# Feed-forward matmuls that alternate between output tiles

## The chip, the cores and the metric

The kernel runs on one core of a Trainium2 chip. The time is device microseconds of one execution. The core has TensorE (matmuls, in the profile PE, its weight loads PEld), VectorE (DVE), ScalarE (ACT), GpSimd (POOL) and SyncE (SP, which issues the DMAs). Each engine works through its own queue in order; they wait for one another through semaphores.

## What is computed

One step of a decoder of two layers, for 256 prompt tokens and 8 sequences of 8 new tokens: 320 columns in all, model width 1024. Each layer has a token mixer (gated linear recurrence beside sparse attention) and a feed-forward part. The change touches the latter alone:

```python
def conv_ffn(h, conv_past, w_gate_up, conv_w, conv_b, w_down):
    g, u = jnp.split(h @ w_gate_up, 2, axis=-1)
    ...
    conv = lax.conv_general_dilated(gfull, ...) + conv_b     # causal, 3 taps, per channel
    out = (jax.nn.gelu(conv) * u) @ w_down
    return out, gfull[:, -(CONV_W - 1):]
# per layer:
    ff, c_st = conv_ffn(rmsnorm(x, norm_ffn[l]), conv_past, ...)
    x = x + ff
```

The feed-forward width is 2816, 22 tiles of 128 channels.

## The kernel before, in words

Channels lie on partitions and the 320 tokens on the free axis. A float32 product is made of three products in fp32r: weights and activations are each split into a high part and a low part (the rest), and `split_products` (L773) issues high x high, high x low and low x high into one output tile. Each of them is one weight load and one matmul of 128x128 on 128x320. The sum over the input channels runs over eight (gate and up) or 22 (down) such triples, all into the same PSUM bank.

PSUM has eight banks, in two sets of four: `MM` (in the trace "mm") and `AXR` ("ax"). Each set is used in rotation by a plan written out by hand (`mm_plan`, `ax_plan`): a tile takes the bank of the tile four places before it in its plan, and `begin` (L689) makes TensorE wait until that one has been emptied. For gate and up the plan is g0, u0, g1, u1, ..., then dn0_0 to dn0_3. So g(j) and u(j) take the banks of g(j-2) and u(j-2), and the four tiles of the first half of down take those of g20, u20, g21, u21. The tiles of the second half, dn1_0 to dn1_3, lie in the other set, behind the last branch products and `norm2`.

Weights come by DMA into a ring of four slots. A part of a slot that is split at once is a unit. For gate and up a unit is both tiles j (2048 columns); for down it is two to four input tiles times four output tiles (1024 to 2048 columns). ScalarE writes a unit's high part (L1353, in the trace L1329 work_parts<-ring) into one of two buffers, once TensorE has read the unit two before; VectorE then puts the low part in the unit's place in the slot (L1690, in the trace L1693). TensorE waits for that (`w_low`) ahead of each unit.

TensorE's order in the feed-forward part (L1265 to L1303): for each of 22 passes j it waits for the unit, runs gate tile j (24 matmuls), then up tile j (24); behind gate tile 0 stands the sum of squares `norm2` (`square_sums`), from which ScalarE makes the scale of all the columns. Then come the units of down, first half (output tiles 0 to 3), then second half (4 to 7). In a unit the order is input tile k, in it output tile m, three products for each; only the last unit of a layer goes output tile by output tile.

In pass j VectorE (L2205 to L2234) splits unit j+1, multiplies gate by the scale (L2215, L2216, which empties the gate bank), makes the low part of the activation j-1 (`act_rest`, L2096), multiplies up by the scale (L2222, which empties the up bank), adds the two other taps of the convolution (L2226, L2228), and after the gelu takes the product with up (L2234). ScalarE (L1611 to L1626) makes the middle tap once gate is emptied, then the high part of unit j+2, then the gelu, then the activation's high part; in the first pass it has the logarithm and exponential of the scale ahead of these and a table load ahead of the gelu. GpSimd copies the borders of the convolution. For down, TensorE waits for activation k ahead of the first output tile of each input tile, in the first half.

The lines at which the order is set:

```python
for j in range(NJ):
    u = FFU + j
    pe.wait_ge(w_low[L], u + 1)
    split_tile(MM[L], f"g{j}", u, 0, h_high, h_low, (h_lo[L], 1) if j == 0 else None)
    if j == 0:
        square_sums()
    split_tile(MM[L], f"u{j}", u, 1, h_high, h_low)
```

Of the kernel before, what the change touches and what calls it, by code (L numbers as in the profile page):

```python
# [45 lines left out]
KD = D // P  # L46
SMP = NSEQ * STEPS
T = SEQ + SMP
DFF = 2816
NJ = DFF // P  # L50
# [183 lines left out]
def hybrid_step(nc, x_prompt, x_sample, cache_cmp, cache_slc, cache_win, state_hgrn, state_conv, page_table, norm_mix,  # L234
# [4 lines left out]
    with ctx:  # L239
# [61 lines left out]
        def part(buf, at, cols):  # L301
            return buf[:, at:at + cols]

        def heads(at):
# [22 lines left out]
        ring_r = nc.alloc_sbuf_tensor_at("ring_low", [P, NSLOT * SLOT], F32R, offset=ring_at)  # L327
# [5 lines left out]
        h_low = nc.alloc_sbuf_tensor_at("h_low", [P, KD * T], F32R, offset=hT_at)[:, :].rearrange(  # L333
            "p (k t) -> p k t", k=KD)
        h_high = part(work_r, 1280 + 2 * UNIT_COLS, KD * T).rearrange("p (k t) -> p k t", k=KD)
# [3 lines left out]
        act_high, act_low = (part(act_r, NJ * T * n, NJ * T).rearrange("p (j t) -> p j t", j=NJ) for n in range(2))  # L339
# [43 lines left out]
        def unit_of(u, buf):  # L383

            b, a, n = SPLIT[u]
            s = (BNO[b] % NSLOT) * SLOT
            if b[:2] in ("ff", "mg", "wo") or b in BY_HEAD:
                v = buf[:, s:s + SLOT].rearrange("p (k h c) -> p k h c", k=KD, h=4)
                return v[:, :, 2 * a:2 * a + 2, :] if b[0] == "w" else v[:, :, a::2, :]
            return buf[:, s + 512 * a:s + 512 * (a + n)].rearrange("p (k h c) -> p k h c", k=n, h=4)  # L390

        def unit_high(u):

            b, _, n = SPLIT[u]
            at = 1280 + UNIT_COLS * (u % 2)
            h = 4 if b[:2] in ("dn", "br") or b in ("w_hi", "w_kvn") else 2
            return work_r[:, at:at + n * h * P].rearrange("p (k h c) -> p k h c", k=n, h=h)
# [19 lines left out]
        def lsem(name):  # L417
            return [sem(f"{name}_{l}") for l in range(DEPTH)]
# [4 lines left out]
        h_hi, h_lo, stored = lsem("h_high"), lsem("h_low_ready"), lsem("outputs_stored")  # L423
        mm_full, mm_act, mm_dve = lsem("mm_full"), lsem("mm_emptied_by_act"), lsem("mm_emptied_by_dve")
# [12 lines left out]
        conv_ready, gelu_ready, act_ready = lsem("conv_ready"), lsem("gelu_ready"), lsem("act_ready")  # L437
# [12 lines left out]
        MM, AXR = [], []  # L450
# [235 lines left out]
        def _(pe):  # L686
            L = 0

            def begin(R, name):  # L689
                w = R.vacant(name)  # L690
                if w:
                    pe.wait_ge(*w)
                return R.bank(name)

            def mm(out, lhsT, rhs, start, stop):
                return nc.tensor.matmul(out, lhsT, rhs, start=start, stop=stop)  # L696

            def tr(out, in_):
                return nc.tensor.transpose(out, in_, ident[0:in_.shape[0], 0:in_.shape[0]])  # L699
# [73 lines left out]
            def split_products(out, high, low, x_high, x_low, start, stop):  # L773

                mm(out, high, x_high, start, False)
                mm(out, high, x_low, False, False)
                return mm(out, low, x_high, False, stop)

            def split_tile(R, name, u, h, x_high, x_low, tile_ready=None, between=None):

                bank = begin(R, name)
                kn = SPLIT[u][2]
                for k in range(kn):
                    if tile_ready is not None:
                        pe.wait_ge(tile_ready[0], tile_ready[1] + k + 1)
                    if between is not None and k == kn // 2:
                        between()
                    last = split_products(bank[:, 0:T], unit_high(u)[:, k, h, :], unit_of(u, ring_r)[:, k, h, :],
                                          x_high[:, k, :], x_low[:, k, :], k == 0, k == kn - 1)
                last.then_inc(R.full, 1)  # L790
# [290 lines left out]
            def layer(l):  # L1081

                nonlocal L
                L = l
# [30 lines left out]
                for x in range(2):  # L1115
                    bank = begin(AXR[L], f"kt{x}")
                    if x == 0:
                        pe.wait_ge(k_roped[L], 3)
                    for i in range(3):
                        last = tr(bank[:, P * i:P * i + TM[i]], stok[0:TM[i], i, 256 * x:256 * x + P])  # L1120
# [6 lines left out]
                banks = [begin(AXR[L], "hidk"), begin(AXR[L], "hidv")]  # L1127
# [7 lines left out]
                for j in range(16):  # L1135
                    for v in range(2):
                        rows = cmpT[:, j % 8, 2 * v:2 * v + 2, :, j // 8:j // 8 + NCB].rearrange(
                            "p g s n -> p (g s) n")
                        last = mm(banks[v][64 * v:64 * v + 64, 0:2 * NCS * NCB], w1[:, v, j, :], rows, j == 0, j == 15)
                        if j == 15:  # L1140
                            last.then_inc(ax_full[L], 1)
                for hb in range(2):
                    bank = begin(AXR[L], f"gsel{hb}")
# [6 lines left out]
                bank = begin(AXR[L], "kcm")  # L1150
                pe.wait_ge(hid_ready[L], 2)
                w2 = slot("w_cmp")
                for g in range(KVH):
                    last = mm(bank[64 * g:64 * g + 64, 0:NCS * NCB], w2[0:64, 2048:2048 + ND],
                              hid[0:64, g].rearrange("p s n -> p (s n)"), True, True)
                last.then_inc(ax_full[L], 1)
                for n in range(3):
                    bank = begin(AXR[L], f"vc{n}")
                    for y in range(6):
                        q, g = (6 * n + y) // 2, (6 * n + y) % 2  # L1160
                        last = mm(bank[0:NCB, ND * y:ND * y + ND], hid[64:128, g, q, :], w2[64:128, 2048:2048 + ND], True,
                                  True)
# [3 lines left out]
                for h in range(HH):  # L1166
                    bank = begin(AXR[L], f"krt{h}")
                    for i in range(3):
                        last = tr(bank[0:TM[i], P * i:P * i + P], kL[:, h, P * i:P * i + TM[i]])
# [24 lines left out]
                for hb in range(2):  # L1194
                    pe.wait_ge(*landed_at(f"kv{hb}", l))
                    kv = slot(f"kv{hb}").rearrange("p (w s a c) -> p w s a c", w=2, s=4, a=2)
                    for x in range(4):
                        w, bp = x // 2, x % 2
                        bank = begin(AXR[L], f"skt{hb}_{x}")
                        for y in range(4):  # L1200
                            last = tr(bank[:, P * y:P * y + P], kv[:, w, 2 * bp + y // 2, y % 2, 0:P])
# [6 lines left out]
                    for c in (2 * hb, 2 * hb + 1):  # L1208
                        bank = begin(AXR[L], f"ds{c}")
# [4 lines left out]
                        for h in range(HH):  # L1214
                            last = mm(bank[:, P * h:P * h + P], krP[rows, h, c // 2, :],
                                      vH[rows, c // 2, P * h:P * h + P], True, True)
# [5 lines left out]
                    n = 4 + 2 * hb  # L1222
# [27 lines left out]
                for n in range(2):  # L1250
                    for y, src, low in ((1, oN_high, oN_low), (0, oH_high, oH_low)):
                        u = MGU + 4 * n + 3 - y
# [8 lines left out]
                for m in range(KD):  # L1261
                    u = WOU + m // 2
                    pe.wait_ge(w_low[L], u + 1)
                    split_tile(MM[L], f"wo{m}", u, m % 2, m_high, m_low, (m_lo[L], 0) if m == 0 else None)
                for j in range(NJ):  # L1265
                    u = FFU + j
                    pe.wait_ge(w_low[L], u + 1)
                    split_tile(MM[L], f"g{j}", u, 0, h_high, h_low, (h_lo[L], 1) if j == 0 else None)
                    if j == 0:
                        square_sums()  # L1270
                    split_tile(MM[L], f"u{j}", u, 1, h_high, h_low)
                for u in down_units:
                    b, a, kn = SPLIT[u]
                    mh, n = int(b[2]), int(b[4:])
                    R = (MM[L], AXR[L])[mh]
                    final = u == len(SPLIT) - 1
                    if u == len(SPLIT) - 2 and l + 1 < DEPTH:
                        params_turned(l + 1)
                    pe.wait_ge(w_low[L], u + 1)
                    k0 = sum(DOWN[mh][:n]) + a  # L1280
                    tiles = [(k0 + kk, m) for kk in range(kn) for m in range(4)]
                    for k, m in sorted(tiles, key=lambda t: t[1]) if final else tiles:
                        bank = begin(R, f"dn{mh}_{m}") if k == 0 else R.bank(f"dn{mh}_{m}")
                        if mh == 0 and m == 0:
                            pe.wait_ge(act_ready[L], k + 1)
                        last = split_products(bank[:, 0:T], unit_high(u)[:, k - k0, m, :],
                                              unit_of(u, ring_r)[:, k - k0, m, :],
                                              act_high[:, k, :], act_low[:, k, :], k == 0, k == NJ - 1)
                        if k == NJ - 1:
                            last.then_inc(R.full, 1)  # L1290
                        if final and k == NJ - 1 and l == DEPTH - 1:
                            if m == 1:
                                turned_back(0, (0, 1, 2, 3))
                                end_sums((0, 1, 2, 3))
                            if m == 2:
                                end_sums((4, 5))
                                turned_back(1, (4, 5))
                            if m == 3:
                                end_sums((6,))
                                turned_back(1, (6,))  # L1300
                    if u in down_inner:
                        last.then_inc(down_read[L], 1)
# [6 lines left out]
            for k in range(KD):  # L1309
                bank = begin(PRO, f"x{k}")  # L1310
                for i in range(3):
                    last = tr(bank[:, P * i:P * i + TM[i]], xin[0:TM[i], i, P * k:P * k + P])
                last.then_inc(pro_full, 1)
            bank = begin(PRO, "low")
            tr(bank[:, 0:16], attb[0:16, 0:P]).then_inc(pro_full, 1)
            params_turned(0)
            for l in range(DEPTH):
                layer(l)
# [1198 lines left out]
```

## Time and profile before

| | |
|---|---|
| median of 3 runs | 1156.46 us (1153.97 to 1159.42) |
| the profiled execution: time, span | 1153.79 us, 1152.0 us |
| granted TensorE clock, mean | 0.985 |
| TensorE matmuls busy | 1125.9 us, 98% of the span |
| weight loads busy | 1023.6 us, 89% |
| VectorE, ScalarE, GpSimd busy | 62%, 47%, 17% |
| HBM read and written | 156.16 MB, 12.46 MB |

The profile is one execution. Busy time of an engine is a mean over all stages, and matmuls overlap in the records (a matmul of 0.31 us starts every 0.15 us), so the pace is to be read from start times, not from durations. The chain of waits says which engine set the end. "L696" is the helper line through which all matmuls pass, L1329 the one of ScalarE; the names of the tiles tell them apart.

### The profile page before, as it was taken

What the parts mean: (1) busy time and instruction counts of PE and PEld (TensorE: products, weight loads), DVE (VectorE), ACT (ScalarE), POOL (GpSimd) and SP (SyncE); (2) the same over time, 40 slices, a digit from 0 to 9 for tenths busy, and PEclk for the clock granted to TensorE, in tenths of its full rate; (3) what the DMA queues carried; (4) which work ended last, traced back from release to release, by engine and by line L of the source; (5) the groups of instructions that cost most, each with busy time, mean ns of one, the idle gap of its engine ahead of it and who ended that gap; (6) DMA issues with size and microseconds to landing.
All of it is one profiled execution on the core that took longest, in us unless ns stands there. A gap on an engine that the chain in (4) does not pass through costs nothing.

```text
span 1152.0 us, 20868 instructions
## 1 busy us (share of the span) xinstructions
PE 1125.9 (98%) x8473; PEld 1023.6 (89%) x8473; DVE 710.1 (62%) x1305; ACT 545.8 (47%) x867; POOL 192.8 (17%) x318
## 2 busy tenths in 40 slices
PE   6999999999999999999999999999999999999997
PEld 5988766778999999999999787776899999999997
DVE  5798165557567777763578835545656677777343
ACT  4543365553356555542444335655434555555232
POOL 2156300012121000100024560000312101100000
PEclk8999999989999999999999999999899999999998
DMA  9556331347644444344456535223684444432411
GB/s 295 160 156 217 110 95 52 111 120 219 220 147 146 147 147 148 114 141 163 146 124 208 184 97 158 74 68 114 177 266 152 149 153 155 155 124 92 168 41 46
DMA packets 151749, 165.90 MB, mean 144 GB/s; under 512 B 31596, under 2 KB 114406, under 8 KB 151398
## 3 DMA queue, kind: packets, MB, share of 16 engines
q1 hardware_dynamic: 151654, 164.58, 45.6%
q8 instruction: 67, 1.10, 0.4%
q14 instruction: 28, 0.23, 0.1%
HBM read 156.16 MB, written 12.46 MB: 146 GB/s over the span
## 4 chain that ended last, share of the span: by engine, by line
PE 92%; DVE 3%; DMA 2%; ACT 1%; issue 1%; SPq 1%; DVEq 0%; ACTq 0%
PE mm L696 65%; PE ax L696 23%; PE ax L699 3%; DMA ring<-in_state_hgrn 1%; ACT mixb L1329 1%; DVE ring_low L1693 1%; DMA ring<-in_state_conv 1%; ACT work_parts L1329 0%; SPq L498 0%; DVE mixb L1848 0%; DVE mixb L2127 0%; DVE work_parts L2096 0%; PE mm L699 0%; DVE cstT L1755 0%; DVE mixb L1865 0%
## 5 line engine op out<-in xcount | busy, mean ns | idle before, releaser
L696 PE MATMUL mm<-work_parts 128*128 128x320 f32 (+1 forms) x1088 | 345.7, 318 | 6.4 <-DVE h_low L1687 4.1
L1693 DVE TENSOR_TENSOR ring_low<-ring,work_parts 128x2048 fp32r<-128x2048 f32 (+2 forms) x116 | 256.0, 2207 | 128.3 <-ACT work_parts L1329 127.9
L696 PE MATMUL mm<-h_low,work_parts 128*128 128x320 f32 x1024 | 321.0, 313 | 0.0
L696 PE MATMUL mm<-work_parts,ring_low 128*128 128x320 f32 x1024 | 317.2, 310 | 0.0
L1329 ACT ACTIVATE work_parts<-ring 128x2048 fp32r<-128x2048 f32 (+2 forms) x116 | 212.2, 1829 | 152.6 <-PE mm L696 82.4
L696 PEld LDWEIGHTS mm<-work_parts 128*128 128x128 f32 x1088 | 206.5, 190 | 13.0 <-issue 7.0
L696 PEld LDWEIGHTS mm<-h_low,work_parts 128*128 128x128 f32 x1024 | 194.5, 190 | 0.3
L696 PEld LDWEIGHTS mm<-work_parts,ring_low 128*128 128x128 f32 x1024 | 194.6, 190 | 0.0
L696 PE MATMUL ax<-act_parts,work_parts 128*128 128x320 f32 x544 | 126.1, 310 | 0.6 <-DVE ring L2118 0.6
L696 PE MATMUL mm<-act_parts,work_parts 128*128 128x320 f32 x480 | 117.2, 309 | 0.0
L696 PE MATMUL mm<-hT,ring 128*128 128x320 f32 x384 | 109.6, 437 | 0.0
L696 PEld LDWEIGHTS mm<-hT,ring 128*128 128x128 f32 x384 | 70.7, 190 | 28.4 <-issue 1.4
L696 PEld LDWEIGHTS ax<-act_parts,work_parts 128*128 128x128 f32 x544 | 92.1, 188 | 2.5 <-DVE ring_low L1693 2.2
L696 PE MATMUL mm<-act_parts,ring_low 128*128 128x320 f32 x304 | 93.9, 309 | 0.0
L696 PE MATMUL ax<-act_parts,ring_low 128*128 128x320 f32 x304 | 93.9, 309 | 0.0
L1329 ACT ACTIVATE attb<-attb,prm 128x256 f32<-128x256 f32 x88 | 41.3, 517 | 93.1 <-DVE attb L2216 93.1
L696 PEld LDWEIGHTS mm<-act_parts,work_parts 128*128 128x128 f32 x480 | 82.9, 188 | 0.4 <-DVE merged_low L2096 0.4
L2387 POOL TENSOR_TENSOR ring<-ring,mixb 128x1024 f32<-128x1024 f32 x8 | 15.2, 1912 | 250.8 <-PE ax L696 250.8
L696 PEld LDWEIGHTS ax<-act_parts,ring_low 128*128 128x128 f32 x304 | 57.1, 188 | 0.0
L696 PEld LDWEIGHTS mm<-act_parts,ring_low 128*128 128x128 f32 x304 | 57.1, 188 | 0.0
L1329 ACT ACTIVATE attb<-ax 128x512 f32<-128x512 f32 (+4 forms) x56 | 34.4, 675 | 41.9 <-PE ax L699 36.0
L2222 DVE TENSOR_TENSOR attb<-mm,work 128x320 f32<-128x320 f32 x44 | 21.6, 491 | 48.6 <-PE mm L696 48.6
(247 smaller groups left out, 1589.5 us busy)
## 6 DMA issues: line engine op xcount, KB each, us to landing
ring<-in_w_gate_up SPq DMA_DIRECT2D x44, 1024.0 KB, 7.0
ring<-in_w_in SPq DMA_DIRECT2D x10, 2048.0 KB, 7.9
ring<-in_w_in SPq DMA_DIRECT2D x18, 1024.0 KB, 5.9
ring<-in_w_down SPq DMA_DIRECT2D x8, 1536.0 KB, 6.7
ring<-in_w_out SPq DMA_DIRECT2D x4, 2048.0 KB, 13.2
ring<-in_w_down SPq DMA_DIRECT2D x4, 2048.0 KB, 7.9
ring<-in_w_in SPq DMA_DIRECT2D x32, 128.0 KB, 3.5
ring<-in_cache_cmp_kv SPq DMA_DIRECT2D x32, 128.0 KB
```

The costliest lines, as they stand in the source:

```text
L696: return nc.tensor.matmul(out, lhsT, rhs, start=start, stop=stop)
L699: return nc.tensor.transpose(out, in_, ident[0:in_.shape[0], 0:in_.shape[0]])
L1329: return nc.scalar.activation(out, in_, f, **kw)
L1693: V.tensor_tensor(unit_of(u, ring_r), unit_of(u, ring), unit_high(u).bitcast(F32), ALU.subtract).then_inc(*st.up(w_low[l]))
L2222: V.tensor_tensor(ut, bank[:, 0:T], rs[:, 0:T], ALU.mult).then_inc(*st.up(mm_dve[L]))
L2387: G.tensor_tensor(s0, s0, end.to_broadcast([P, NSEQ, HD]), ALU.mult).then_inc(*st.up(decayed[L]))
```

## The change

Two helpers are added. `across_tiles` issues the three products pass by pass: high x high into every tile of a list, then high x low into every tile, then low x high. `split_pair` does this for gate tile j and up tile j; both banks are asked for first, and both are reported full at the end. The sum of squares of the first pass stands behind the pair. In down, all units but a layer's last go input tile by input tile across the four output tiles, the four banks are asked for at the first input tile, and the wait for an activation stands ahead of that.

```diff
+            def across_tiles(banks, highs, lows, x_high, x_low, start, stop):
+
+                out = []
+                for n, (weights, x) in enumerate(((highs, x_high), (highs, x_low), (lows, x_high))):
+                    out = [mm(bank[:, 0:T], w, x, start and n == 0, stop and n == 2) for bank, w in zip(banks, weights)]
+                return out
+
+            def split_pair(names, u, x_high, x_low, tile_ready=None):
+
+                banks = [begin(MM[L], name) for name in names]
+                for k in range(KD):
+                    if tile_ready is not None:
+                        pe.wait_ge(tile_ready[0], tile_ready[1] + k + 1)
+                    ends = across_tiles(banks, [unit_high(u)[:, k, h, :] for h in range(2)],
+                                        [unit_of(u, ring_r)[:, k, h, :] for h in range(2)], x_high[:, k, :],
+                                        x_low[:, k, :], k == 0, k == KD - 1)
+                for last in ends:
+                    last.then_inc(mm_full[L], 1)
...
-                    split_tile(MM[L], f"g{j}", u, 0, h_high, h_low, (h_lo[L], 1) if j == 0 else None)
+                    split_pair((f"g{j}", f"u{j}"), u, h_high, h_low, (h_lo[L], 1) if j == 0 else None)
                     if j == 0:
                         square_sums()
-                    split_tile(MM[L], f"u{j}", u, 1, h_high, h_low)
...
-                    tiles = [(k0 + kk, m) for kk in range(kn) for m in range(4)]
-                    for k, m in sorted(tiles, key=lambda t: t[1]) if final else tiles:
+                    for k in range(k0, k0 if final else k0 + kn):
+                        if mh == 0:
+                            pe.wait_ge(act_ready[L], k + 1)
+                        ends = across_tiles([begin(R, f"dn{mh}_{m}") if k == 0 else R.bank(f"dn{mh}_{m}") for m in range(4)],
+                                            [unit_high(u)[:, k - k0, m, :] for m in range(4)],
+                                            [unit_of(u, ring_r)[:, k - k0, m, :] for m in range(4)],
+                                            act_high[:, k, :], act_low[:, k, :], k == 0, k == NJ - 1)
+                        last = ends[-1]
+                        if k == NJ - 1:
+                            for end in ends:
+                                end.then_inc(R.full, 1)
+                    for k, m in [(k, m) for m in range(4) for k in range(k0, k0 + kn)] if final else []:
```

## Rows read from the trace of the kernel before

**Rows 1.** The page: TensorE's share of the span, and the chain that ended last

```profile
PE 1125.9 (98%) x8473; PEld 1023.6 (89%) x8473; DVE 710.1 (62%) x1305; ACT 545.8 (47%) x867; POOL 192.8 (17%) x318
...
PE 92%; DVE 3%; DMA 2%; ACT 1%; issue 1%; SPq 1%; DVEq 0%; ACTq 0%
```

**Rows 2.** The chain in order of time, both layers: start us, us, what

```profile
350.22 190.07 PE mm L696 x1296
...
906.70 190.07 PE mm L696 x1296
```

**Rows 3.** Windows, TensorE: us, PE busy (x), granted clock, DMA share, GB/s

```profile
353.58:501.42 147.84, 147.84 (x1010) 1.00 0.40 132
```

**Rows 4.** Timeline, TensorE, passes 0 and 1: start us, us, line, operation

```profile
346.00 0.31 PE L696 MATMUL mm<-work_parts 128*128 128x320 f32 x1
...
349.52 0.70 PE L696 MATMUL ax<-mixb,consts 128*128 128x320 f32 x2
...
353.58 0.30 PE L696 MATMUL mm<-work_parts 128*128 128x320 f32 x1
```

**Rows 5.** Timeline, ScalarE, passes 0 and 1

```profile
350.26 0.53 ACT L1329 ACTIVATE work<-ax,epsb 128x320 f32<-128x320 f32 x1 [0.80 <-PE ax L696]
350.82 0.47 ACT L1329 ACTIVATE work<-work 128x320 f32<-128x320 f32 x1
...
353.78 1.92 ACT L1329 ACTIVATE work_parts<-ring 128x2048 fp32r<-128x2048 f32 x1 [0.55 <-PE mm L696]
355.72 1.28 ACT L1329 ACT_TABLE_LOAD   x1
357.02 0.47 ACT L1329 ACTIVATE attb<-attb 128x320 f32<-128x320 f32 x1
...
360.72 0.94 ACT L1329 ACTIVATE attb<-attb,prm 128x256 f32<-128x256 f32 x2 [2.19 <-DVE attb L2216]
361.56 1.90 ACT L1329 ACTIVATE work_parts<-ring 128x2048 fp32r<-128x2048 f32 x1
```

**Rows 6.** Timeline, VectorE, passes 0 to 2

```profile
357.52 0.49 DVE L2234 TENSOR_TENSOR attb<-attb 128x320 f32<-128x320 f32 x1 [1.95 <-ACT attb L1329]
357.93 2.29 DVE L1693 TENSOR_TENSOR ring_low<-ring,work_parts 128x2048 fp32r<-128x2048 f32 x1
360.13 0.42 DVE L2215 TENSOR_TENSOR attb<-mm,work 128x256 f32<-128x256 f32 x1
...
361.00 0.49 DVE L2222 TENSOR_TENSOR attb<-mm,work 128x320 f32<-128x320 f32 x1
361.69 0.48 DVE L2226 SCALAR_TENSOR_TENSOR attb<-attb,prm 128x256 f32<-128x256 f32 x1 [0.21 <-ACT attb L1329]
...
362.81 0.28 DVE L2228 SCALAR_TENSOR_TENSOR attb<-attb,prm 128x64 f32<-128x64 f32 x1
...
364.26 2.29 DVE L1693 TENSOR_TENSOR ring_low<-ring,work_parts 128x2048 fp32r<-128x2048 f32 x1
```

**Rows 7.** Timeline, TensorE, behind the longest wait for a DMA

```profile
246.68 0.87 PE L696 MATMUL ax<-ring,mixb 128*32 128x128 f32 x16 [2.19 <-DMA ring<-in_state_hgrn]
```

**Rows 8.** Timeline, ScalarE and VectorE in down: splits of units

```profile
506.89 1.50 ACT L1329 ACTIVATE work_parts<-ring 128x1536 fp32r<-128x1536 f32 x1 [0.63 <-PE mm L696]
...
508.42 1.76 DVE L1693 TENSOR_TENSOR ring_low<-ring,work_parts 128x1536 fp32r<-128x1536 f32 x1 [1.90 <-ACT work_parts L1329]
...
528.01 1.07 ACT L1329 ACTIVATE work_parts<-ring 128x1024 fp32r<-128x1024 f32 x1 [3.78 <-PE mm L696]
```

**Rows 9.** Timeline, TensorE and VectorE: first matmuls of down, up 21

```profile
501.42 0.45 PE L696 MATMUL mm<-act_parts,work_parts 128*128 128x320 f32 x2
...
501.62 0.49 DVE L2222 TENSOR_TENSOR attb<-mm,work 128x320 f32<-128x320 f32 x1 [1.68 <-PE mm L696]
```

**Rows 10.** Windows, TensorE, as rows 3, behind the wait of rows 7

```profile
247.00:253.00 6.00, 6.00 (x109) 0.50 1.07 253
253.00:257.00 4.00, 4.00 (x19) 0.50 0.11 32
```

## The prediction

> **What bounds the kernel now.** I read the page's busy shares first, then the chain, then the chain in order of time, then the matmuls' own start times. TensorE works for 98% of the span and has one weight load for each matmul; 92% of the chain that ended last lies on it [rows 1]. In order of time, each of the two feed-forward stages is one unbroken piece of 190.07 us and 1,296 matmuls [rows 2], at a granted clock of 1.00 [rows 3], the higher of the two levels (2.4 GHz). So nothing releases TensorE here: its pace is the time, and every new wait in front of it is paid in full. VectorE and ScalarE are busy for 62% and 47%; what matters is not that share but how much of their work lies between the end of one pass and the start of the pass after next.
>
> **The pace.** Between the first matmul of pass 1 and the first of the down projection lie 21 pairs of 48 matmuls: 501.42 - 353.58 = 147.84 us, so 146.67 ns each [rows 4, 9]. There a matmul changes bank once in 24. The down projection changes bank once in 3. Its units of 36 matmuls are timed by ScalarE, which starts a split when the unit before has been read: four of them take 528.01 - 506.89 = 21.12 us, or 144 matmuls of 146.67 ns [rows 8]. 48 bank changes against about 6 differ by less than the 0.01 us to which a row is written, so a change of bank costs or gives under 0.01/42 = 0.24 ns. That is the main reason for my forecast: if a matmul had to wait for the one before it in the same bank, the down projection would already run faster.
>
> **The change, part by part.** It touches 22 x 48 = 1,056 matmuls of gate and up per layer and 480 of the 528 in down (the last unit, 4 x 4 x 3 = 48, keeps its order), 3,072 in both layers.
> - Order of the products. No matmul or weight load is added or removed. The same weights no longer come twice in a row, but each matmul has its load already [rows 1]. Most likely 0 ns; by the bound above +-0.24 ns x 3,072 = +-0.7 us. The far bound is 320 columns at 2.4 GHz, 133.3 ns, which no row shows as a pace.
> - The gate tile of a pass is now filled together with the up tile, half a pass (3.52 us) later. What VectorE and ScalarE did to gate while TensorE worked on up must now fit in the pass after. The trace has this very case: in pass 1 VectorE comes late and does everything in one run. From its first read of gate (360.13) to the start of the split of the next weights (364.26) it takes 4.13 us, and the split 2.29, 6.42 in all [rows 6]. With 0.03 us for a hand-over (ScalarE's 357.02 + 0.47 to VectorE's 357.52 [rows 5, 6]), 6.45 us. TensorE wants these weights one pass of 7.04 us after the fill, less the 0.20 us by which it issues ahead of it (501.42 against 501.62 [rows 9]): 6.84. Slack 0.39 us, so no wait in the steady passes. Cost 0; what hides it is the pass itself, and 0.39 us is all there is to lose.
> - The first pass of a layer. The sum of squares (norm2) moves from behind gate 0 to behind up 0. Pass 0 starts at 346.00, so norm2 is issued at 346.00 + 7.04 = 353.04 in place of 349.52 [rows 4]. Pass 1 still starts at 353.58. The logarithm follows 0.74 us after norm2 (350.26 - 349.52 [rows 4, 5]): 353.78; the exponential 0.56 later, 0.47 long [rows 5]: 354.81. VectorE reads gate at 354.84. ScalarE's convolution start comes 0.59 after that read (360.72 - 360.13 [rows 5, 6]): 355.43, the split's high part 0.84 later: 356.27, the table load of the gelu 1.94 after that: 358.21, the gelu 1.30 later: 359.51 [rows 5]. The taps (ready 1.40 us after 356.40, by 361.69 to 362.81 + 0.28 [rows 6]) are earlier and hide. The product follows at 360.01, the split of unit 2 at 360.42, ready at 362.71 [rows 6], TensorE at 362.74. It wants it at 353.58 + 7.04 = 360.62. **Wait: 2.12 us.** Next late is unit 3: VectorE begins gate 1 at 360.42 + 2.20 = 362.62 (the step 357.93 to 360.13), done at 369.04, wanted at 362.74 + 7.04 = 369.78: no second wait.
> - The start of down. The four banks are now asked for before the first matmul. The fourth was up 21, which was filled last; until now it was asked for 9 matmuls (1.32 us) later, and gate 21 had half a pass. Fill at 501.62, VectorE reads up 0.87 us behind the start of gate and takes 0.49 (361.00 - 360.13 [rows 6]): 502.98, TensorE 503.01, wanted 501.42 [rows 9]. **Wait: 1.59 us.** Behind this wait stand all of down and nothing of another queue: the weight loads of the slots are released by ends of passes, which only shift. Unit 2 of down is split by 501.62 + 4.13 + 1.76 = 507.51 at the latest and wanted at 508.29. I take 1.76 from a split of that size [rows 8].
> - In the second half of down (banks of the other set) the tiles asked for are those of the branch products and norm2, long empty: 0. The four fills at the end of a half come within 4 matmuls in place of 9 before; their reader comes later: 0. The wait for an activation stays ahead of each input tile: 0.
> Sum: 2 x (2.12 + 1.59) = +7.4 us. On the profiled execution (1153.79, span 1152.00) that is 1161.2. The median of the three runs shown is 2.67 above it, so I put the forecast at 1156.46 + 7.4 = **1163.9 us**, +0.64%.
>
> **The clock.** A gap in front of TensorE can cost more than itself. After the longest one, 2.19 us [rows 7], the granted clock was 0.50, the lower level (1.2 GHz), from about 247 to 257 us [rows 10]. Around that gap stand small matmuls (128x128 on 32 columns of the array), here stand full ones; so I take 0. Bound: with dense work behind, as in 253 to 257, 4 us at the half clock lose about 4 x (1 - 0.55) = 1.8 us per gap (0.55 = 146.67 / 266.7, 320 columns at 1.2 GHz), 7.2 for four. The Trainium skill, "TensorE: Matmul & The Clock Gate", section on psum-queue depth-cycling, goes further: a kernel that cycled through its banks each iteration had its clock fall and rise again and again, from short idle times between groups. By that rule the steady passes too would lose. The trace does not agree so far: with four banks in rotation the clock is 1.00 over the whole stage [rows 3].
>
> **The rivals.**
> - *Clock* (0.07). The four new gaps each bring the half clock: 1163.9 + 7.2 = 1171.1. For it: both the drop above and its length; against: one core in dense work.
> - *Chain longer than the pass* (0.05). VectorE's run of 6.45 us decides from 6.84 on. If the splits or reads were 10% slower under new overlaps, 7.1 us, each of some 40 passes would wait 0.25 us: +10, 1174. Against it: pass 1 has the same overlaps already.
> - *Smaller waits* (0.17). If the table load ran before ScalarE's split chain, its 1.30 us would leave the first wait: 0.82 + 1.59 twice, +4.8, 1161.3, within 0.5%. Against it: it follows the split at once [rows 5].
> - *Banks matter after all* (0.09), the other side: two matmuls in a row into one bank hinder one another, and only true alternation frees them. At 133.3 ns a pair takes 6.40 us, but then VectorE's chain binds: a pass starts every 6.45 + 0.20 = 6.65 us, 0.39 less than 7.04. 20 passes x 0.39 = 7.8, down 480 x 13.3 ns = 6.4, two layers 28.4, less 7.4: 1156.5 - 21.0 = 1135.5. It decides from 7.4 / 3,072 = 2.4 ns per matmul on, ten times the bound of the pace. That compiled order stays as before is not a case of its own: TensorE takes matmuls in program order, and it would show as no change.
>
> **How the numbers follow.** The main case has 0.62. A measurement of this kernel can tell about 0.5%, 5.8 us, from no change. The main case is only 1.6 us beyond it, so of its 0.62 I give 0.06 to "same". Slower: 0.56 + 0.07 + 0.05 = 0.68; same: 0.17 + 0.06 = 0.23; faster: 0.09. The range goes from no waits at all (1156.0) to the clock rival (1171.1, rounded up to 1172.0); it leaves out the bank case and the long chain, 0.14, and the far ends of the clock case.
>
> **What would show it.** Right: in the chain, the stage in three pieces with about 2.1 us before pass 2 (releaser VectorE's split, L1693) and 1.6 before down (releaser VectorE's read of up, L2222), 7.04 us from pass to pass, 5.28 per unit in down, clock 1.00. Wrong: pairs under 7.00 us (banks matter), a wait at each pass (chain too long), 0.50 in the clock behind the gaps, or a table load ahead of the split.

## The result, and the profile after

| | before | changed |
|---|---|---|
| median of 5 runs | 1156.46 us (1153.97 to 1159.42) | 1162.44 us (1161.46 to 1167.69) |
| ratio | | 1.0068, 95% interval 1.0044 to 1.0091 |
| profiled execution, time | 1153.79 us | 1167.69 us |
| its span, its mean granted clock | 1152.0 us, 0.985 | 1165.9 us, 0.981 |

The change makes the kernel slower by 0.7%; forecast were 1163.9 us and +0.64%. The profiled execution is the slowest of its five, so its span is not the result, but its waits can be read. Lines of the code have moved: the split is L1721 (was L1693), the read of up L2250 (L2222), the read of gate L2243 (L2215), ScalarE's helper L1357 (L1329).

The page of the changed kernel: busy shares, the chain by engine, and the two groups of matmuls in which the new idle time lies (the first had 6.4 us of it before, the second none). Columns of a group: count, busy us, mean ns, idle time before, and what ended it:

```profile
PE 1133.7 (97%) x8473; PEld 1030.6 (88%) x8473; DVE 714.0 (61%) x1305; ACT 539.4 (46%) x867; POOL 192.9 (17%) x318
...
PE 90%; DVE 4%; ACT 2%; DMA 2%; issue 1%; SPq 1%; DVEq 0%; ACTq 0%
...
L696 PE MATMUL mm<-work_parts 128*128 128x320 f32 (+1 forms) x1088 | 289.6, 319 | 10.1 <-DVE ring_low L1721 5.7
...
L696 PE MATMUL mm<-act_parts,work_parts 128*128 128x320 f32 x480 | 98.6, 309 | 2.9 <-DVE attb L2250 2.9
```

The counts are those of [rows 1]: nothing was added or taken away. TensorE's share of the chain fell from 92 to 90%, and VectorE and ScalarE gained it. The chain in order of time shows where (start us, us, what; first layer's feed-forward part):

```profile
349.69 0.55 PE ax L696 x2
...
352.86 1.80 ACT work_parts L1357
354.68 1.28 ACT L1357
356.97 2.21 DVE ring_low L1721
359.23 143.51 PE mm L696 x959
504.34 38.95 PE mm L696 x264
```

The unbroken 190.07 us of [rows 2] have become three pieces. Between the sum of squares (349.69) and 359.23 the end of the kernel hangs on ScalarE and VectorE, though TensorE is still at work on pass 1 for most of it; and down begins anew at 504.34. TensorE's timeline around both waits, the first from the second layer and the second from the first (in brackets the idle time and its releaser):

```profile
921.32 0.46 PE L696 MATMUL mm<-work_parts,ring_low 128*128 128x320 f32 x2
923.66 0.56 PE L696 MATMUL mm<-work_parts 128*128 128x320 f32 x2 [1.89 <-DVE ring_low L1721]
```

```profile
502.42 0.46 PE L696 MATMUL mm<-work_parts,ring_low 128*128 128x320 f32 x2
504.34 0.38 PE L696 MATMUL mm<-act_parts,work_parts 128*128 128x320 f32 x1 [1.46 <-DVE attb L2250]
```

Two matmuls start every 0.295 us here, so without a wait the next would have started at 921.62 and 502.72. The waits cost 2.04 and 1.62 us, counted from start to start in this way; the bracket is shorter, since it counts from the end of the last matmul. The first wait's chain, on ScalarE (scale, high part of unit 2, table load, gelu):

```profile
350.27 0.53 ACT L1357 ACTIVATE work<-ax,epsb 128x320 f32<-128x320 f32 x1 [4.27 <-PE ax L696]
350.83 0.47 ACT L1357 ACTIVATE work<-work 128x320 f32<-128x320 f32 x1
351.92 0.93 ACT L1357 ACTIVATE attb<-attb,prm 128x256 f32<-128x256 f32 x2 [0.62 <-DVE attb L2244]
352.76 1.90 ACT L1357 ACTIVATE work_parts<-ring 128x2048 fp32r<-128x2048 f32 x1
354.68 1.28 ACT L1357 ACT_TABLE_LOAD   x1
355.98 0.47 ACT L1357 ACTIVATE attb<-attb 128x320 f32<-128x320 f32 x1
```

and on VectorE:

```profile
351.33 0.42 DVE L2243 TENSOR_TENSOR attb<-mm,work 128x256 f32<-128x256 f32 x1 [3.01 <-ACT work L1357]
...
356.48 0.49 DVE L2262 TENSOR_TENSOR attb<-attb 128x320 f32<-128x320 f32 x1 [2.19 <-ACT attb L1357]
356.89 2.28 DVE L1721 TENSOR_TENSOR ring_low<-ring,work_parts 128x2048 fp32r<-128x2048 f32 x1
```

VectorE sits idle for 3.01 us. Both tiles are full soon after norm2 starts, at 349.53, and from there on it waits for the scale alone. From norm2's start to TensorE's restart it is 923.66 - 913.97 = 9.69 us in the second layer (norm2 started at 913.97); the prediction's steps add up to 362.74 - 353.04 = 9.70.

One thing is not as forecast: the pace of the steady passes. VectorE's reads of up, 16 passes apart:

```profile
383.12 0.48 DVE L2250 TENSOR_TENSOR attb<-mm,work 128x320 f32<-128x320 f32 x1
...
496.61 0.48 DVE L2250 TENSOR_TENSOR attb<-mm,work 128x320 f32<-128x320 f32 x1
```

113.49 / 16 = 7.093 us per pass, 0.053 more than before. No wait stands in them: within a pass every pair of matmuls takes 0.295 us instead of 0.293. Pass 0 is the exception, it takes 6.99 us from its first matmul to norm2 (906.98 to 913.97), 0.05 less than before. Down, which alternates as well, runs at its old pace. ScalarE's splits of its units, four units of 36 matmuls apart:

```profile
515.17 1.49 ACT L1357 ACTIVATE work_parts<-ring 128x1536 fp32r<-128x1536 f32 x1 [3.79 <-PE mm L696]
...
536.29 1.06 ACT L1357 ACTIVATE work_parts<-ring 128x1024 fp32r<-128x1024 f32 x1 [4.22 <-PE mm L696]
```

21.12 us, to the hundredth the time of [rows 8]. And the clock: windows behind the first wait (us, PE busy, granted clock, DMA share, GB/s), three of the first layer, one of the second.

```profile
359.00:361.00 2.00, 1.77 (x8) 0.70 1.03 343
361.00:363.00 2.00, 2.00 (x9) 0.50 1.07 366
363.00:365.00 2.00, 2.00 (x15) 0.94 0.91 289
924.00:926.00 2.00, 2.00 (x16) 1.00 1.07 370
```

In the first layer the clock was at half for some 3.4 us behind the wait, in the second it stayed at 1.00, behind the same wait.

The second layer, at the full clock throughout, shows the sum of the terms, from the first matmul of pass 0 to the first of down:

```profile
906.98 0.46 PE L696 MATMUL mm<-work_parts 128*128 128x320 f32 x2
...
1067.24 0.96 PE L696 MATMUL mm<-act_parts,work_parts 128*128 128x320 f32 x5 [1.46 <-DVE attb L2250]
```

That is 160.26 us, against 501.42 - 346.00 = 155.42 in the kernel before [rows 4, 9]: 4.84 more. Of these, 2.04 + 1.62 = 3.66 are the waits and 21 x 0.053 - 0.05 = 1.06 the pace; the first matmuls behind a wait take the remaining 0.1. For both layers it makes 7.3 us of waits and 2.1 of pace, 9.7 with that remainder. The two profiled spans differ by 13.9; 1.5 us of the rest are the half clock behind the first wait, and what is left lies outside of the feed-forward part, where the two executions had the lower clock in different stretches.

**How the clock is taken out.** Each execution lists its mean granted clock. Over the 64 executions of the kernel before that stood beside the experiments (1147.13 to 1161.89 us), a straight line through time against clock falls by 9.4 us per 0.01 of clock, and 1.5 us of scatter remain around it. Below, "at equal clock" is the mean of a kernel's executions above that line, with its standard error. The changed kernel stands 8.5 +- 1.0 us above (5 executions), in accord with 9.7. This way of comparing also takes out whatever clock the change itself costs. The mean clocks hardly differ (0.983 before, 0.984 changed, 0.982 for the kernel with pairs alone), but so few executions would not show a loss of 0.001 or 0.002, which is 1 to 2 us.

### The profile page after: what moved, and what is told of

Same layout as the page of the kernel before. It is cut to its first block, busy times and chain, and to the rows that moved or that the text cites. A ratio compares the mean times of both kernels' runs of the same rounds, so it can differ in the third digit from the quotient of the medians.

```text
span 1165.9 us, 20876 instructions
## 1 busy us (share of the span) xinstructions
PE 1133.7 (97%) x8473; PEld 1030.6 (88%) x8473; DVE 714.0 (61%) x1305; ACT 539.4 (46%) x867; POOL 192.9 (17%) x318
## 4 chain that ended last, share of the span: by engine, by line
PE 90%; DVE 4%; ACT 2%; DMA 2%; issue 1%; SPq 1%; DVEq 0%; ACTq 0%
PE mm L696 64%; PE ax L696 23%; PE ax L699 3%; DVE ring_low L1721 1%; DMA ring<-in_state_hgrn 1%; ACT mixb L1357 1%; DMA ring<-in_state_conv 1%; ACT work_parts L1357 1%; SPq L498 0%; DVE mixb L1876 0%; DVE mixb L2155 0%; ACT work L1357 0%; PE mm L699 0%; DVE work_parts L2124 0%; DVE cstT L1783 0%
## 5 line engine op out<-in xcount | busy, mean ns | idle before, releaser
L1721 DVE TENSOR_TENSOR ring_low<-ring,work_parts 128x2048 fp32r<-128x2048 f32 (+2 forms) x116 | 256.0, 2207 | 129.5 <-ACT work_parts L1357 129.1
L696 PE MATMUL mm<-work_parts 128*128 128x320 f32 (+1 forms) x1088 | 289.6, 319 | 10.1 <-DVE ring_low L1721 5.7
L1357 ACT ACTIVATE work_parts<-ring 128x2048 fp32r<-128x2048 f32 (+2 forms) x116 | 211.3, 1822 | 130.3 <-PE ax L696 69.3
L696 PE MATMUL mm<-h_low,work_parts 128*128 128x320 f32 x1024 | 263.3, 313 | 0.0
L696 PE MATMUL mm<-work_parts,ring_low 128*128 128x320 f32 x1024 | 261.5, 311 | 0.0
L696 PEld LDWEIGHTS mm<-work_parts 128*128 128x128 f32 x1088 | 191.6, 189 | 17.1 <-DVE ring_low L1721 6.8
L696 PEld LDWEIGHTS mm<-work_parts,ring_low 128*128 128x128 f32 x1024 | 181.4, 190 | 0.0
L696 PEld LDWEIGHTS mm<-h_low,work_parts 128*128 128x128 f32 x1024 | 179.7, 190 | 0.2
L696 PE MATMUL mm<-act_parts,work_parts 128*128 128x320 f32 x480 | 98.6, 309 | 2.9 <-DVE attb L2250 2.9
L1357 ACT ACTIVATE attb<-attb,prm 128x256 f32<-128x256 f32 x88 | 41.1, 514 | 126.8 <-DVE attb L2244 126.8
L696 PE MATMUL ax<-act_parts,ring_low 128*128 128x320 f32 x304 | 77.4, 312 | 0.0
L696 PE MATMUL mm<-act_parts,ring_low 128*128 128x320 f32 x304 | 72.6, 309 | 0.0
L1357 ACT ACTIVATE attb<-ax 128x512 f32<-128x512 f32 (+4 forms) x56 | 34.3, 673 | 42.5 <-PE ax L699 36.6
L2448 POOL COPY work<-attb 128x2 f32<-128x2 f32 x44 | 16.3, 370 | 206.5 <-DVE attb L2244 206.5
```

The source lines that it names most:

```text
L1357: return nc.scalar.activation(out, in_, f, **kw)
L1721: V.tensor_tensor(unit_of(u, ring_r), unit_of(u, ring), unit_high(u).bitcast(F32), ALU.subtract).then_inc(*st.up(w_low[l]))
L2448: G.tensor_copy(glast_p[:, :, j - 1], gp[:, SEQ:SEQ + 2])
```

## The experiments

My theory behind the result: two new waits per layer, plus a pace term of 0.053 us per alternating pass of gate and up (from pass 1 on). Rivals: that the order of the products costs most of it, or that the waits come from something other than norm2's place and the banks.

**Both waits taken away.** Pass 0, pass 21 and the first input tile of down have the old order, all else alternates.

```diff
-                    split_pair((f"g{j}", f"u{j}"), u, h_high, h_low, (h_lo[L], 1) if j == 0 else None)
-                    if j == 0:
-                        square_sums()
+                    if 0 < j < NJ - 1:
+                        split_pair((f"g{j}", f"u{j}"), u, h_high, h_low)
+                    else:
+                        split_tile(MM[L], f"g{j}", u, 0, h_high, h_low, (h_lo[L], 1) if j == 0 else None)
+                        if j == 0:
+                            square_sums()
+                        split_tile(MM[L], f"u{j}", u, 1, h_high, h_low)
...
+                    if u == DNU:
+                        for m in range(4):
+                            bank = begin(R, f"dn0_{m}")
+                            if m == 0:
+                                pe.wait_ge(act_ready[L], 1)
+                            split_products(bank[:, 0:T], unit_high(u)[:, 0, m, :], unit_of(u, ring_r)[:, 0, m, :],
+                                           act_high[:, 0, :], act_low[:, 0, :], True, False)
-                    for k in range(k0, k0 if final else k0 + kn):
+                    for k in range(k0 + (u == DNU), k0 if final else k0 + kn):
```

> The alternation is kept for passes 1 to 20 and for down from its second input tile on; pass 0, pass 21 and the first input tile of down have the old order, so neither new wait should be there. Theory (two new waits per layer, 2.05 and 1.62 us, plus 0.054 us per alternating pass): only the second term stays, 2 x 20 x 0.054 = +2.2 us over the kernel before, ratio about 1.002. Rival (the order of the products or a lower clock makes most of the loss, the waits little): +6 to +8 us, ratio 1.005 to 1.007. Rival (nothing but the waits): +0.

Measured: ratio 1.0035 (1.0010 to 1.0061), 12 executions; at equal clock +2.1 +- 0.4 us. No wait for up or for a split stands in the feed-forward stages; the waits for a split that are left are one of 1.9 us in all, against 5.7 in three. Passes take (458.16 - 387.23) / 10 = 7.093 us:

```profile
387.23 0.48 DVE L2261 TENSOR_TENSOR attb<-mm,work 128x320 f32<-128x320 f32 x1
...
458.16 0.48 DVE L2261 TENSOR_TENSOR attb<-mm,work 128x320 f32<-128x320 f32 x1
```

The chain in order of time has the stage in one piece again, with the count of [rows 2]:

```profile
347.42 191.14 PE mm L696 x1296
```

191.14 - 190.07 = 1.07 us more per layer, which is 20 passes x 0.053. About three quarters of the loss were the waits, and the pace term is the rest.

**Gate and up alone.** The old loop of down is put back, the pairs stay.

```diff
-                    for k in range(k0, k0 if final else k0 + kn):
...
+                    tiles = [(k0 + kk, m) for kk in range(kn) for m in range(4)]
+                    for k, m in sorted(tiles, key=lambda t: t[1]) if final else tiles:
...
```

> Gate and up alternate, down in the old order. Theory: wait before pass 2 stays (2.05 us), of the wait before down only what up 21 is late for the fourth tile stays (1.56 - 9 x 0.147 = 0.24 us), pace term 22 x 0.054 = 1.19 us per layer: 2 x 3.48 = +7.0 us. Rival (the wait before down is the larger part): under +4.

Measured: 1.0060 (1.0037 to 1.0083), at equal clock +6.5 +- 0.5 us. The small wait of the fourth tile is there too: 506.63 and one matmul of 0.147 would be 506.78; it came at 506.99, 0.21 us later against 0.24 expected:

```profile
506.63 0.31 PE L696 MATMUL mm<-act_parts,ring_low 128*128 128x320 f32 x1
506.99 0.56 PE L696 MATMUL mm<-act_parts,work_parts 128*128 128x320 f32 x2
```

**Down alone.** Gate and up in the old order, down as changed.

```diff
-                    split_pair((f"g{j}", f"u{j}"), u, h_high, h_low, (h_lo[L], 1) if j == 0 else None)
+                    split_tile(MM[L], f"g{j}", u, 0, h_high, h_low, (h_lo[L], 1) if j == 0 else None)
                     if j == 0:
                         square_sums()
+                    split_tile(MM[L], f"u{j}", u, 1, h_high, h_low)
```

> Gate and up in the old order, down alternates. Theory: the first matmul of down waits until VectorE has emptied up 21, which it reads at once: 0.20 + 0.49 + 0.03 = 0.72 us per layer, no pace term in down: +1.4 us, within what can be told from no change. Rival (alternation in down makes matmuls faster or slower by 1 ns each): 960 x 1 ns = 1 us to either side of that, seen in the period of its units (5.24 or 5.32 instead of 5.28 us).

Measured: 1.0015 (0.9994 to 1.0036), at equal clock +1.5 +- 0.3 us. The wait is short, as forecast: counted from start to start, 502.75 - 501.76 - 0.15 = 0.84 us against 0.72.

```profile
502.75 1.41 PE L696 MATMUL mm<-act_parts,work_parts 128*128 128x320 f32 x8 [0.68 <-DVE attb L2251]
```

Units keep 5.28 us. This experiment and the last add up to 8.0, near the 8.5 of both together: of the wait of 1.62 us before down, 0.84 comes from asking for all four banks at once. The rest is there only when gate and up fill together: gate 21, the low part of the activation before it and up 21 then stand in front of VectorE one behind the other.

**norm2 moved alone.** The kernel before with the sum of squares behind up 0; nothing alternates.

```diff
                     split_tile(MM[L], f"g{j}", u, 0, h_high, h_low, (h_lo[L], 1) if j == 0 else None)
-                    if j == 0:
-                        square_sums()
                     split_tile(MM[L], f"u{j}", u, 1, h_high, h_low)
+                    if j == 0:
+                        square_sums()
```

> The kernel before with one edit: norm2 stands behind up 0 instead of behind gate 0; nothing alternates. Theory (the wait before pass 2 comes from the place of norm2, since the scale is what VectorE waits for): the same wait of 2.05 us before pass 2 in each layer, none before down, passes of 7.04 us: +4.1 us at the same granted clock. Rival (the wait comes from gate and up filling together): no wait, +0.

Measured: 1.0024 (1.0004 to 1.0044), 12 executions, at equal clock +3.9 +- 0.3 us. Its wait, second layer:

```profile
915.92 0.31 PE L696 MATMUL mm<-work_parts,ring_low 128*128 128x320 f32 x1
918.18 0.41 PE L696 MATMUL mm<-work_parts 128*128 128x320 f32 x1 [1.96 <-DVE ring_low L1693]
```

918.18 - 915.92 - 0.15 = 2.11 us. The place of one sum, 0.53 us of TensorE's time, makes about half of what the change costs, with no alternation at all.

**norm2 in the middle of pass 0.** The changed kernel, with the sum at its old time.

```diff
                 for k in range(KD):
...
+                    if tile_ready is not None and k == KD // 2:
+                        square_sums()
...
-                    if j == 0:
-                        square_sums()
```

> The changed kernel, but norm2 stands in the middle of pass 0 (where it stood before) instead of behind it. Theory: the scale is ready before the tiles are full, so the chain in front of unit 2 starts with the fill: read of gate 0.20 us after the end of the pass, +0.59 +0.84 +1.94 +1.30 +0.50 +0.41 +2.29 +0.03 = 8.10 us behind the point at which pass 1 was to start, against 7.09 for pass 1: wait of about 1.0 us in place of 2.05, so 2 x 1.0 = 2.1 us less than the changed kernel. Rival (the table load of the gelu alone sets that wait, wherever norm2 stands): still 2.05.

Measured: 1.0058 (1.0035 to 1.0082), 12 executions, at equal clock +5.4 +- 0.5, so 3.1 +- 1.1 us less than the changed kernel, where 2.1 were expected. The wait:

```profile
361.88 0.46 PE L696 MATMUL mm<-work_parts,ring_low 128*128 128x320 f32 x2
363.15 0.56 PE L696 MATMUL mm<-work_parts 128*128 128x320 f32 x2 [0.81 <-DVE ring_low L1721]
```

363.15 - 361.88 - 0.29 = 0.98 us against 1.0 expected. What is left fits the late fill of gate 0, from which the chain of the expectation starts. But its passes were a surprise, 69.86 / 10 = 6.986 us, in both layers:

```profile
385.23 0.48 DVE L2250 TENSOR_TENSOR attb<-mm,work 128x320 f32<-128x320 f32 x1
...
455.09 0.48 DVE L2250 TENSOR_TENSOR attb<-mm,work 128x320 f32<-128x320 f32 x1
```

From pass 1 on, TensorE's instructions are the same as in the changed kernel. How many of the 12 executions had this faster pace isn't known, so the 5.4 us can't be split between waits and pace. Three ways of ordering the products, and repeats, were to say what sets this pace.

**One bank, the weights apart.** The kernel before with the second and third product exchanged.

```diff
-                mm(out, high, x_low, False, False)
-                return mm(out, low, x_high, False, stop)
+                mm(out, low, x_high, False, False)
+                return mm(out, high, x_low, False, stop)
```

> The kernel before, with the three products of every triple in the order high x high, low x high, high x low: the same weights never twice in a row, all three in one bank as before. If the slower pace of the alternating passes (7.09 us for 48 matmuls in place of 7.04) comes from weights that are no longer used twice in a row: 7.09 here. If it comes from a bank that is written again after one other: 7.04, and the time as before. If it comes from two matmuls in a row that stream the same activations: in between, about 7.07 (one in three instead of one in two).

Measured: 1.0003 (0.9977 to 1.0030), passes of 7.04 us (70.40 us for ten). So the second use of the same weights in a row gave nothing that could be measured.

**Both tiles open, the bank changed once in three.** In `split_pair`:

```diff
-                    ends = across_tiles(banks, [unit_high(u)[:, k, h, :] for h in range(2)],
...
+                    ends = [split_products(banks[h][:, 0:T], unit_high(u)[:, k, h, :], unit_of(u, ring_r)[:, k, h, :],
+                                           x_high[:, k, :], x_low[:, k, :], k == 0, k == KD - 1) for h in range(2)]
```

> The changed kernel, but in gate and up each input tile has the three products of gate, then the three of up: both tiles still fill together, the bank changes once in three. Pace by all of the theories on the order of the single products: 7.04 us. If it is the two open tiles, or VectorE's and ScalarE's other timing beside the pass: 7.09. The waits before pass 2 and before down stay at 2.1 and 1.6 us in each case.

One execution, 1171.70 us at a clock of 0.974. Passes 70.39 / 10 = 7.039 us, and both waits are there (1.96 us idle before pass 2, 1.33 us before down, from start to start). The two open tiles and the other timing of VectorE and ScalarE are not the cause of the pace.

**Banks alternate, the products staggered.** In `split_pair`:

```diff
...
+                    mm(b[0], high[0], xh, first, False)
+                    mm(b[1], high[1], xl, first, False)
+                    mm(b[0], low[0], xh, False, False)
+                    mm(b[1], high[1], xh, False, False)
+                    ends = [mm(b[0], high[0], xl, False, end), mm(b[1], low[1], xh, False, end)]
```

> The changed kernel, but in gate and up the banks alternate while the products are staggered: gate high x high, up high x low, gate low x high, up high x high, gate high x low, up low x high. Bank written again after one other: 7.09 us. Weights used only once: 7.09. The same activations streamed twice in a row (here one in six, in the changed kernel one in two): about 7.06.

One execution, 1165.11 us. Passes of 7.04 us in both layers (70.40 for ten), with the bank changed at every matmul. With this, none of the three theories holds as I put it: the weights are never used twice in a row and a bank is written again after one other, at the old pace; and in the experiment before last the same activations came twice in a row once in three, at the old pace too.

**Down two by two.** The changed kernel, with `across_tiles` called for tiles 0 and 1, then for 2 and 3.

```diff
-                        ends = across_tiles([begin(R, f"dn{mh}_{m}") if k == 0 else R.bank(f"dn{mh}_{m}") for m in range(4)],
...
+                        for two in (range(0, 2), range(2, 4)):
+                            ends += across_tiles([begin(R, f"dn{mh}_{m}") if k == 0 else R.bank(f"dn{mh}_{m}") for m in two],
...
```

> The changed kernel, but down alternates between two tiles at a time instead of four. If it is a bank that is written again after one other that costs 1.1 ns: units of 36 matmuls take 5.32 us in place of 5.28. If the slower pace belongs to gate and up alone (their operands): 5.28.

One execution, 1166.89 us; units of down 5.28 us. Down now has the very order of products that gate and up have, over two tiles, and keeps the old pace of 146.67 ns: the order alone does not make the other pace. Its passes of gate and up, unchanged code, differ between the layers, 70.93 us for ten in the first and 69.87 in the second:

```profile
386.26 0.48 DVE L2252 TENSOR_TENSOR attb<-mm,work 128x320 f32<-128x320 f32 x1
...
457.19 0.48 DVE L2252 TENSOR_TENSOR attb<-mm,work 128x320 f32<-128x320 f32 x1
...
947.93 0.48 DVE L2252 TENSOR_TENSOR attb<-mm,work 128x320 f32<-128x320 f32 x1
...
1017.80 0.48 DVE L2252 TENSOR_TENSOR attb<-mm,work 128x320 f32<-128x320 f32 x1
```

**Two kernels once more, unchanged.** Is the pace a property of the program?

> The changed kernel once more, to see whether the pace of its alternating passes belongs to the program or to the execution. If to the program: 7.09 us per pass in both layers again. If it is settled at each start behind a wait: 6.99 us in at least one layer is possible, as in the second layer of the kernel with down by two tiles.

1172.46 us at a clock of 0.978; 7.09 us in both layers, waits of 1.89 and 1.46 us idle as before.

> The kernel with norm2 in the middle of pass 0 once more. If the pace belongs to the program: 6.99 us per pass in both layers again. If it is settled at each start: 7.09 us in at least one layer is possible.

1161.42 us. The same program that ran at 6.986 us per pass now ran at 7.093:

```profile
383.98 0.48 DVE L2250 TENSOR_TENSOR attb<-mm,work 128x320 f32<-128x320 f32 x1
...
454.91 0.49 DVE L2250 TENSOR_TENSOR attb<-mm,work 128x320 f32<-128x320 f32 x1
```

So it belongs to the execution. The alternating order of gate and up has two paces, 147.8 and 145.6 ns per matmul. It is not settled for a whole stage either: it changes at interruptions, and nowhere else. The second layer of the kernel with down two by two has both:

```profile
908.22 0.45 PE L696 MATMUL mm<-work_parts,ring_low 128*128 128x320 f32 x2
...
914.33 0.45 PE L696 MATMUL mm<-work_parts,ring_low 128*128 128x320 f32 x2
914.63 0.70 PE L696 MATMUL ax<-mixb,consts 128*128 128x320 f32 x2
...
917.25 0.46 PE L696 MATMUL mm<-h_low,work_parts 128*128 128x320 f32 x2
...
921.68 0.46 PE L696 MATMUL mm<-h_low,work_parts 128*128 128x320 f32 x2
...
929.76 0.45 PE L696 MATMUL mm<-h_low,work_parts 128*128 128x320 f32 x2
...
939.37 0.45 PE L696 MATMUL mm<-h_low,work_parts 128*128 128x320 f32 x2
```

In pass 0, 42 matmuls take 6.11 us, 145.5 ns each. Behind norm2 (914.63), in pass 1, 30 take 4.43 us, 147.7 ns. Behind the wait before pass 2, 66 take 9.61 us, 145.6 ns, and so on to the end of the stage. All 12 profiled stages whose pass 0 alternates have the fast pace in it up to norm2 and the slow one from there to the wait; the wait is followed by the slow one in nine and by the fast one in three. In the two stages without the waits, pass 1 begins with the slow pace, and it stays. That is 11 of 14 with the slow pace in their steady passes. The clock is not what chooses: in the stage shown the granted clock was 0.50 from 926 to 929, behind the wait, and on both sides of that a pair of matmuls takes 0.29 us; other stages were at 1.00 throughout and had the slow pace. What does choose, and why down has neither pace in the same order, was not found.

## Why the prediction was right, point by point

- *What bounds the kernel.* TensorE, and new waits paid in full: so it was. The two waits, sized 7.4 us for both layers, measured 7.3. Taking them away left +2.1 +- 0.4 of +8.5 +- 1.0 us.
- *First pass.* Forecast 2.12 us, measured 2.04; the chain was right to 0.01 us, and the wait came out shorter mostly because pass 1 took 7.09 us. The cause, norm2's new place, is shown by moving it alone (+3.9 us) and by moving it back (wait 0.98).
- *Start of down.* Forecast 1.59 us, measured 1.62, releaser VectorE's read of up 21, as said.
- *Steady passes.* No wait in any of them: VectorE's run of 6.45 us fits. The split starts 464.41 - 460.28 = 4.13 us behind the read of gate, as in [rows 6], and the slack of 0.39 us was enough even for passes of 6.99 us.
- *Order of the products.* This is the step that was mis-sized: I bounded it by +-0.24 ns from the changes of bank in down, and it was +1.1 ns in most stages of gate and up, -1.1 in some, 0 in down. The bound was sound for a change of bank, which it measured (the staggered order and down confirm it), but I used it for another thing, a new sequence of bank, weights and activations together. It was worth 2.1 us of the 8 to 10 in the profiled execution.
- *Clock.* I took 0, with a bound. In a single execution it was wrong: behind the wait before pass 2 the half clock came in 9 of the 14 stages with the full-length wait, and cost 8.99 - 7.45 = 1.5 us (time between the reads of up of passes 1 and 2 in the first and second layer of the changed kernel), against 1.8 in the bound. It never came behind the wait of 0.98 us (4 stages), nor behind a wait before down (0.74 to 1.62 us, 16 stages). At 9 in 14 this is an estimated 2 x 9/14 x 1.5 = 1.9 us per execution, or 0.002 of mean clock; the mean clocks of so few executions neither show nor exclude it. What the Trainium skill says on the page "TensorE: Matmul & The Clock Gate", section on psum-queue depth-cycling, is not borne out here as far as the rotation goes: the staggered order changes the bank at every matmul, and its clock was 1.00 even behind the wait before pass 2. The short idle times between groups that the section blames fit in part: within the feed-forward stages the clock fell only behind the wait before pass 2, and not behind each of them.
- *The rivals.* Banks matter after all: excluded, down is not faster by 0.01 us in 144 matmuls, and the staggered order not by 0.01 us in a pass. Smaller waits through an earlier table load: it stands right behind the split, at 354.68.
- *The signs named beforehand.* Both waits, their releasers and 5.28 us in down came as said; 7.04 us from pass to pass and a clock of 1.00 behind the waits did not.
- The median came 1.5 us under the forecast, well within the scatter that the clock makes. That +0.64% met +0.68% so closely is partly luck: the interval goes from +0.44 to +0.91%, 5 to 10.5 us, and the forecast left out two terms of some 2 us each, pace and clock, which at this scatter do not show in the median. What was not luck is the two waits.

## What to carry to other kernels

When a TensorE-bound stage merges two output tiles into one pass, list who reads the tile that used to be ready half a pass earlier, and look at the first and the last pass by themselves: in the steady passes there was slack, and both waits were at the edges. A small matmul whose result scales everything behind it (here a sum of squares) should keep its place in time when the work around it is regrouped. Alternating banks from one matmul to the next bought nothing that could be relied on: in down and in the staggered order nothing, in gate and up a pace that was slower in 11 stages and faster in three.

## What the runs showed that was not expected

The pace of a dense stream of matmuls is not a constant of its shape. For the same 128x128 by 128x320 matmuls it was 146.67 ns in the old order, in down, and in the blocked and the staggered order; in the alternating order of gate and up it was 147.8 or 145.6 ns, with no wait in between. It changed from one to the other only behind an interruption (norm2, or the wait before pass 2), and behind the wait it differed between layers and executions of one program.

The lower clock level came and went between executions of the same program, and moved the time by 9.4 us per 0.01 of mean clock. That is the larger part of the spread of 1147.13 to 1161.89 us in the kernel before. A wait of 2 us in dense matmuls was followed by some 3.4 us at the half clock in 9 of 14 cases, by none in the other 5.
